# Where the projection matmuls stand in the eight delta rounds of a two-block model

## The chip, the cores and the metric

The kernel runs on one core of one Trainium2 chip. The metric is the device time of one execution in microseconds (us), lower is better. The engines are named as the profile names them: PE (TensorE, with PEld for its weight loads), DVE (VectorE), ACT (ScalarE), POOL (GpSimd) and SP (SyncE, which issues the weight DMAs).

## The reference, cut to what matters

Two transformer-like blocks are applied to 512 positions of width 1024. What the change touches is the gated delta rule in the first block. It runs in two directions over 8 heads, with heads of 128:

```python
lower = where(tri_strict, einsum('cd,sd->cs', k_beta, k) * decay, 0)
sol = triangular_solve(lower, rhs, lower=True, unit_diagonal=True)   # (I + lower)^-1 rhs
v_new = ui - wi @ state
o = qd @ state + qki @ v_new
state = state * exp(gl) + kt.T @ v_new
```

Ahead of it and beside it stand large projections of the same normed input: `proj = h @ w_in` gives the gates, `z`, `q`, `k`, `v` and others, and `y_conv = c @ w_conv_out` follows a depthwise convolution over 31 positions (`depthwise_conv(c, conv_dw_w)`), a layer norm and a silu.

## The kernel before, in words

**Rounds.** The kernel takes 128 positions of 4 heads in both directions at a time: J = 8 problems at once, in 8 rounds R0 to R7 (`delta(R)` on each engine). R0 to R3 are the first four heads, R4 to R7 the last four, and r is the number of the round within its half. In a round PE forms the decay table (L762, pA), the products of k with itself (L767, pB) and of k with q (L773, pA). Then the triangular matrix is inverted by doubling, in 6 levels (`LEVELS`). A level is a product `ub`,`ls` into pC (L746; level 0 uses the identity in `consts`), a copy of it to `yb` by ACT (L1252), then two products, `yb`,`tb` into pC and `tb`,`yb` into pB (L746, in the last level L795), and two subtractions by DVE that renew `ub` (L1723, level 0: L1718, last level: L1726 and L1727 into `en`) and `tb` (L1730). The next level needs the renewed `ub` and a masked matrix `ls` that POOL makes (L2090) between other work of its own. L803 and L810 join the two halves of 64, DVE copies the result (L1747, L1748), and L817, L825 and L827, L835 and L836, and L841 make the new values, the output and the state. DVE adds the output into `oT` (L1757, L1761) and renews the state `st` (L1770).

**Fillers.** A weight unit is a tile of 1024 rows by 128 columns; its product with the 512 positions takes 24 matmuls of 128x512 (L571, into pg), because each fp32 product is made of three fp32r ones (`UNIT` = 24). Four units, 96 matmuls, are handed out over each round: R0 to R3 do the gates, R4 and R5 do `z`, R6 and R7 the convolution's output projection. The table `GAP` says how many of the 96 stand in each of the round's 18 gaps on PE: gap 0 ahead of L773, gap 1 ahead of level 0, gap 2 after level 0, gaps 3 to 12 two to a level (after the first product, and after the other two), gap 13 after L803, gap 14 after L810, gap 15 after L817, gap 16 after the products into pB, gap 17 at the end.

**Taps.** In R0 to R3, called heavy rounds here, DVE also works off the long convolution, tap by tap (L1490, one multiply-add of 128x512). `TAP` gives the number in each gap, 47 a round. They stand in DVE's queue at fixed places: those of gaps 0 and 1 ahead of level 0's `tb` and `ub`, those of gap 17 ahead of the next round's first work (L1693). R4 to R7, the light rounds, have none.

**Weights.** Each unit's weights are split into a rounded part (`w_hi`, ACT, L1020) and a rest (`w_lo`, DVE, L1446), in two slots each. The split for a unit can begin when the unit two before it is finished on PE. DVE does the splits and the evictions at the places that `gap(R, g)` works out from `GAP`: a unit that ends in gap 2 to 16 gets its split at the next odd gap or later, and what ends in gap 15 or 16 is dealt with in gap 17, after the state. In R6 and R7 DVE also evicts the units (`taken`, L1652). pg has two banks, so a unit can begin when the one two before it has been evicted.

Of the kernel before, what the change touches and what calls it, by code (L numbers as in the profile page):

```python
# [34 lines left out]
LEVELS = 6  # L35
# [82 lines left out]
def build(nc, a, out):  # L118

    ctx = ExitStack()  # L120
    with ctx:
# [268 lines left out]
        taps_unit = 8  # L390


        A_, B_ = 4, 4
        GAP = [16, 13, 4] + [A_, B_] * (LEVELS - 1) + [4, 5, 7, 7, 0]
        TAP = [2, 4, 0] + [1, 2] * 2 + [2, 3] * 3 + [0, 4, 5, 6, 5]
        PD = 4
        NORM_AT = 14
        UNIT = 3 * KT
        assert sum(GAP) == 4 * UNIT and taps_unit * (KT - 2) + 3 * HH + 4 * sum(TAP) >= len(TAPS)

# [52 lines left out]
        def parts(R, g):  # L453

            q, end = sum(GAP[:g]), sum(GAP[:g + 1])
            while q < end:
# [984 lines left out]
        def _(dve):  # L1441
# [35 lines left out]
            def taps(count):  # L1477

                for q in range(done_taps[0], min(done_taps[0] + count, len(TAPS))):
                    t, j = TAPS[q]  # L1480
                    src, w = cpad[:, t, j:j + T], vec[:, t, len(VEC) + j:len(VEC) + j + 1]
                    y = csum_in(t)
                    if j == 0:
                        ev_wait(dve, ("gla", t))
                        if 3 <= t < KT - 1:
                            dve.wait_ge(S("tap"), TAPS.index((t - 2, CK - 1)) + 1)
                        ins = dve.tensor_scalar(y, src, w, v("conv_b", t), ALU.mult, ALU.add)
                    else:
                        dve.wait_ge(S("tap"), TAPS.index((t, j - 1)) + 1)
                        ins = dve.scalar_tensor_tensor(y, src, w, y, ALU.mult, ALU.add)  # L1490
                    ins.then_inc(S("tap"), 1)
                done_taps[0] = min(done_taps[0] + count, len(TAPS))
# [164 lines left out]
            def gap(R, g):  # L1657

                n, last = len(GAP), g == len(GAP) - 1
                if g % 2 and g > 1:  # L1660
# [10 lines left out]
                if R < 4:  # L1671
                    taps(TAP[g])

# [571 lines left out]
```

## Time and profile before

| | us |
|---|---|
| median of 3 runs | 2404.41 (2402.77 to 2405.77) |
| the profiled execution | 2404.79 |
| its span | 2402.9 |
| R0 to R3 (248.6 to 530.4) | 66.9, 71.4, 73.7, 69.8 |
| R4 to R7 (641.3 to 881.8) | 56.5, 60.1, 65.1, 58.8 |

A round is counted from the start of L762 to that of the next round's, R3 and R7 to the end of their work on PE. The rounds are 522 us of the span. PE is busy 93% of the span. A matmul's duration in the trace includes its way through the array; what one costs in a row of them is the distance between two starts. A product of fp32 data appears in the trace as two instructions for each one of the program, so that "x32" there is "x16" in the program.

### The profile page before, as it was taken

Reading aid. Unit: us, or ns where it says so; the run is one execution under the profiler, and the core shown is the slowest. Engines: PE = TensorE matmul, PEld = TensorE weight load, DVE = VectorE, ACT = ScalarE, POOL = GpSimd, SP = SyncE. Lnnn points to the kernel's source line nnn. Section 1 sums busy time; section 2 is a strip of 40 time slices with the busy share of each in tenths; the row PEclk is TensorE's granted clock in tenths of the full one; section 3 lists DMA queues with packets and bytes.
Section 4 is the critical chain, followed back from the end, with each engine's and each line's share of the span. In section 5 each row is a group of like instructions: output and inputs, shape, how many; then the busy total and the mean of one; then the engine's idle time right before and its main releaser. Section 6 shows DMA issues by size and latency. Waiting matters only on the chain.

```text
span 2402.9 us, 33875 instructions
## 1 busy us (share of the span) xinstructions
PE 2230.9 (93%) x13850; PEld 1832.4 (76%) x13850; DVE 1304.9 (54%) x1750; ACT 788.9 (33%) x1106; POOL 327.7 (14%) x228
## 2 busy tenths in 40 slices
PE   6999888899899999999999979999988897999996
PEld 4877777778787878888888768888876575888885
DVE  4578798887654446444443354444226835444423
ACT  4345222225433223333322333332223443323221
POOL 0100442130343310100000120000011212000001
PEclk8999899999899999999999979999997986999998
DMA  3232011112111123322232312223221111222321
GB/s 139 82 115 79 28 54 41 45 50 79 36 41 41 54 71 137 122 96 96 96 108 93 105 53 96 96 96 108 96 85 44 36 59 45 97 96 96 111 94 40
DMA packets 54901, 189.68 MB, mean 79 GB/s; under 512 B 6144, under 2 KB 6400, under 8 KB 54784
## 3 DMA queue, kind: packets, MB, share of 16 engines
q1 hardware_dynamic: 51904, 182.75, 22.6%
q10 hardware_dynamic: 2880, 5.24, 0.6%
q8 instruction: 89, 1.46, 0.3%
q14 instruction: 28, 0.23, 0.0%
HBM read 178.53 MB, written 9.44 MB: 78 GB/s over the span
## 4 chain that ended last, share of the span: by engine, by line
PE 77%; DVE 13%; issue 6%; ACT 2%; DMA 1%; SPq 0%; POOL 0%; DVEq 0%; ACTq 0%; POOLq 0%
PE pg L571 65%; PE pC L746 3%; PE pB L602 2%; DVE cpad L1490 2%; DVE w_lo L1446 1%; DVE x L1928 1%; DVE a_lo L1471 1%; PE pB L746 1%; PE pC L609 1%; PE pB L609 1%; DVE oT L1490 1%; DVE sacc L1600 1%; DVE cacc L1490 1%; ACT w_hi L1020 1%; DVE hb L1924 1%
## 5 line engine op out<-in xcount | busy, mean ns | idle before, releaser
L571 PE MATMUL pg<-a_hi,w_hi 128*128 128x512 f32 x1904 | 770.6, 405 | 49.5 <-DVE a_lo L1471 36.2
L571 PE MATMUL pg<-a_hi,w_lo 128*128 128x512 f32 x1904 | 763.8, 401 | 0.0
L571 PE MATMUL pg<-a_lo,w_hi 128*128 128x512 f32 x1904 | 761.9, 400 | 0.0
L1446 DVE TENSOR_TENSOR w_lo<-w_raw,w_hi 128x1024 fp32r<-128x1024 f32 (+3 forms) x299 | 389.1, 1301 | 458.8 <-ACT w_hi L1020 458.7
L1020 ACT ACTIVATE w_hi<-w_raw 128x1024 fp32r<-128x1024 f32 (+3 forms) x299 | 329.6, 1102 | 669.1 <-PE pg L571 648.0
L571 PEld LDWEIGHTS pg<-a_hi,w_hi 128*128 128x128 f32 x1904 | 366.5, 192 | 142.3 <-issue 31.4
L571 PEld LDWEIGHTS pg<-a_hi,w_lo 128*128 128x128 f32 x1904 | 366.6, 193 | 78.4 <-issue 1.3
L571 PEld LDWEIGHTS pg<-a_lo,w_hi 128*128 128x128 f32 x1904 | 367.1, 193 | 74.2 <-issue 0.7
L2073 POOL TENSOR_TENSOR acc<-acc,sq 128x512 f32<-128x512 f32 x64 | 95.1, 1486 | 1368.3 <-ACT sq L1037 1367.4
L571 PE MATMUL pg<-h_hi,w_hi 128*128 128x512 f32 x528 | 208.0, 394 | 0.0
L571 PE MATMUL pg<-h_hi,w_lo 128*128 128x512 f32 x528 | 207.0, 392 | 0.0
L571 PE MATMUL pg<-h_lo,w_hi 128*128 128x512 f32 x528 | 204.9, 388 | 0.0
L1847 DVE TENSOR_TENSOR tmp<-pg,rstd 128x512 f32<-128x512 f32 x66 | 45.7, 692 | 189.3 <-PE pg L571 189.3
L2090 POOL TENSOR_TENSOR ls<-lc,consts 128x512 f32<-128x512 f32 x48 | 74.6, 1561 | 461.5 <-ACT lc L1247 452.9
L571 PEld LDWEIGHTS pg<-h_hi,w_lo 128*128 128x128 f32 x528 | 99.1, 188 | 23.2
L571 PEld LDWEIGHTS pg<-h_lo,w_hi 128*128 128x128 f32 x528 | 99.1, 188 | 22.2
L571 PEld LDWEIGHTS pg<-h_hi,w_hi 128*128 128x128 f32 x528 | 99.3, 188 | 19.7
L1490 DVE SCALAR_TENSOR_TENSOR cpad<-cpad,vec 128x512 f32<-128x512 f32 x120 | 102.0, 911 | 0.2
L1252 ACT ACTIVATE yb<-pC 128x512 f32<-128x512 f32 x40 | 24.0, 599 | 188.1 <-PE pC L746 188.1
L1318 ACT ACTIVATE h_hi<-tmp 128x512 f32 (+1 forms) x66 | 41.7, 632 | 131.7 <-DVE tmp L1851 131.7
L1600 DVE SCALAR_TENSOR_TENSOR sacc<-pad,swt,sacc 128x512 f32<-128x512 f32 x96 | 76.5, 797 | 3.4
L1856 DVE TENSOR_TENSOR h_lo<-tmp,h_hi 128x512 f32 (+1 forms) x66 | 45.7, 692 | 58.3 <-ACT h_hi L1318 58.3
(323 smaller groups left out, 2379.0 us busy)
## 6 DMA issues: line engine op xcount, KB each, us to landing
w_raw<-in_w_gu SPq DMA_DIRECT2D x132, 512.0 KB, 3.3
w_raw<-in_w_in SPq DMA_DIRECT2D x74, 512.0 KB, 3.3
w_raw<-in_w_dn SPq DMA_DIRECT2D x48, 704.0 KB, 4.0
spill_g<-tmp ACTq DMA_DIRECT2D x16, 256.0 KB, 2.0
w_raw<-in_w_co SPq DMA_DIRECT2D x8, 512.0 KB, 3.6
w_raw<-in_w_do SPq DMA_DIRECT2D x8, 512.0 KB, 3.8
w_raw<-in_w_wo SPq DMA_DIRECT2D x8, 512.0 KB, 4.1
w_raw<-in_w_pg SPq DMA_DIRECT2D x8, 512.0 KB, 6.8
```

The lines of the kernel that those rows point to most:

```text
L571: ins = pe.matmul(dst, w_of(w, n % 2, k), b(k), start=first and q == 0, stop=last and q == len(todo) - 1)
L602: ins = pe.matmul(dst[:, c:c + 1], src[:, c * P:(c + 1) * P], ones[:, 0:1], start=q == 0, stop=q == len(srcs) - 1)
L609: ins = pe.matmul(dst[:, c * P:(c + 1) * P], factors[:, c:c + 1].to_broadcast([P, P]), ident, start=True, stop=True)
L746: ins = pe.matmul(dst[s, j, :], lhs[s, j, :], id64[s, :] if rhs is None else rhs[s, j, :], start=True, stop=True)
L1020: act.activation(w_hi[:, n % 2, 0:c], w_raw[:, n % 4, 0:c], ACT.Copy).then_inc(S("w_hi"), 1)
L1446: dve.tensor_tensor(w_lo[:, n % 2, 0:c], w_raw[:, n % 4, 0:c], w_hi[:, n % 2, 0:c].bitcast(F32), ALU.subtract).then_inc(S("w_lo"), 1)
L1490: ins = dve.scalar_tensor_tensor(y, src, w, y, ALU.mult, ALU.add)
L1600: ins = dve.scalar_tensor_tensor(y, src, w, y, ALU.mult, ALU.add)
L1847: dve.tensor_tensor(tmp2[:], bu, rstd[:], ALU.mult).then_inc(S("evD"), 1)
L1856: dve.tensor_tensor(at_m(h_lo), tmp2[:], at_m(h_hi).bitcast(F32), ALU.subtract)\
L2073: pool.tensor_tensor(acc[:], acc[:], sq[:, t % 2, :], ALU.add).then_inc(S("add"), 1)
L2090: pool.tensor_tensor(ls[:, lv % 2].rearrange("p (d h) c -> p d h c", d=2), lc[:].rearrange("p (d h) c -> p d h c", d=2), mask, ALU.mult)\
```

## The change

Two tables of numbers are replaced, and nothing else:

```diff
         taps_unit = 8
 
 
-        A_, B_ = 4, 4
-        GAP = [16, 13, 4] + [A_, B_] * (LEVELS - 1) + [4, 5, 7, 7, 0]
-        TAP = [2, 4, 0] + [1, 2] * 2 + [2, 3] * 3 + [0, 4, 5, 6, 5]
+        GAP = [26, 22, 0] + [0, 0] * (LEVELS - 1) + [10, 10, 14, 14, 0]
+        TAP = [8, 9, 0] + [1, 1] * 5 + [0, 4, 6, 6, 4]
         PD = 4
         NORM_AT = 14
         UNIT = 3 * KT
```

The 96 matmuls of a round now stand as 26 in gap 0, 22 in gap 1, none in gaps 2 to 12, and 10, 10, 14 and 14 in gaps 13 to 16. The 47 taps stand as 8 and 9 in gaps 0 and 1 (2 and 4 before), one in each of gaps 3 to 12 (21 in all before), and 0, 4, 6, 6 and 4 in gaps 13 to 17 (0, 4, 5, 6 and 5 before). All counts and products are the same.

PE in R0, before, one level and the start of the next:

```order
L746 MATMUL pC<-ub,ls 64x64 x16
L571 MATMUL pg<-a_hi,w_lo 128x512
L571 MATMUL pg<-a_hi,w_hi 128x512
L571 MATMUL pg<-a_lo,w_hi 128x512
L571 MATMUL pg<-a_hi,w_lo 128x512
L746 MATMUL pC<-yb,tb 64x64 x16
L746 MATMUL pB<-tb,yb 64x64 x16
L571 MATMUL pg<-a_hi,w_hi 128x512
L571 MATMUL pg<-a_lo,w_hi 128x512
L571 MATMUL pg<-a_hi,w_lo 128x512
L571 MATMUL pg<-a_hi,w_hi 128x512
L746 MATMUL pC<-ub,ls 64x64 x16
```

PE in R0, after, from the end of gap 1 (line numbers are one lower in the changed kernel):

```order
L570 MATMUL pg<-a_hi,w_lo 128x512
L745 MATMUL pC<-consts,ls 64x64 x16
L745 MATMUL pC<-ub,ls 64x64 x16
L745 MATMUL pC<-yb,tb 64x64 x16
L745 MATMUL pB<-tb,yb 64x64 x16
L745 MATMUL pC<-ub,ls 64x64 x16
```

Nothing stands between the products of the levels any more.

DVE in R2, before, from the end of the matrix on (the eight instructions of L1707) to level 1:

```order
L1707 SCALAR_TENSOR_TENSOR en<-pB,gat,en 128x128 x8
L1490 SCALAR_TENSOR_TENSOR cpad<-cpad,vec 128x512 x6
L1716 TENSOR_TENSOR tb<-consts,ls 128x512
L1718 TENSOR_TENSOR ub<-consts,pC 128x512
L1446 TENSOR_TENSOR w_lo<-w_raw,w_hi 128x1024
L1490 SCALAR_TENSOR_TENSOR cpad<-cpad,vec 128x512
L1723 TENSOR_TENSOR ub<-ub,pC 128x512
L1730 TENSOR_TENSOR tb<-tb,pB 128x512
```

and after:

```order
L1706 SCALAR_TENSOR_TENSOR en<-pB,gat,en 128x128 x8
L1489 SCALAR_TENSOR_TENSOR cpad<-cpad,vec 128x512 x17
L1715 TENSOR_TENSOR tb<-consts,ls 128x512
L1717 TENSOR_TENSOR ub<-consts,pC 128x512
L1445 TENSOR_TENSOR w_lo<-w_raw,w_hi 128x1024 x2
L1489 SCALAR_TENSOR_TENSOR cpad<-cpad,vec 128x512
L1722 TENSOR_TENSOR ub<-ub,pC 128x512
L1729 TENSOR_TENSOR tb<-tb,pB 128x512
```

Seventeen taps instead of six now stand ahead of `tb` and `ub`, and both weight splits of the round's first two units stand right behind them.

DVE from the end of R6 to the start of R7, before:

```order
L1761 TENSOR_TENSOR oT<-oT,pA 128x4x128 x2
L1770 SCALAR_TENSOR_TENSOR st<-st,gat,pC 128x128 x8
L1446 TENSOR_TENSOR w_lo<-w_raw,w_hi 128x1024
L1652 TENSOR_TENSOR ya<-pg,tmp_60 128x512
L1693 TENSOR_TENSOR et<-pA,gat 128x512 x2
```

and after:

```order
L1760 TENSOR_TENSOR oT<-oT,pA 128x4x128 x2
L1769 SCALAR_TENSOR_TENSOR st<-st,gat,pC 128x128 x8
L1445 TENSOR_TENSOR w_lo<-w_raw,w_hi 128x1024 x2
L1651 TENSOR_TENSOR ya<-pg,tmp_59 128x512
L1651 TENSOR_TENSOR ya<-pg,tmp_60 128x512
L1692 TENSOR_TENSOR et<-pA,gat 128x512 x2
```

The splits and the evictions (`ya`) of the round's last two units are both at its end now, ahead of the next round's L1692.

## Rows read from the trace of the kernel before

**Rows 1.** The page, part 1: busy time by engine, instructions.
```profile
PE 2230.9 (93%) x13850; PEld 1832.4 (76%) x13850; DVE 1304.9 (54%) x1750; ACT 788.9 (33%) x1106; POOL 327.7 (14%) x228
```

**Rows 2.** By round, R0 to R3, then R5: length, busy PE, PEld, DVE, ACT, POOL, granted clock.
```profile
248.60:315.50 66.90, 59.73 (x737) 50.06 (x737) 59.28 (x80) 20.09 (x27) 24.64 (x16) 0.94 0.12 41
315.50:386.90 71.40, 62.76 (x768) 52.62 (x769) 62.22 (x87) 18.96 (x26) 26.35 (x16) 0.95 0.13 46
386.90:460.60 73.70, 63.43 (x771) 53.18 (x770) 62.95 (x93) 18.96 (x26) 23.58 (x16) 0.93 0.13 44
460.60:530.40 69.80, 59.42 (x755) 49.63 (x753) 63.33 (x94) 17.68 (x25) 20.86 (x14) 0.98 0.14 47
697.80:757.90 60.10, 59.22 (x770) 50.26 (x769) 26.55 (x42) 26.25 (x37) 20.84 (x16) 1.00 0.14 46
```

**Rows 3.** Waits of PE, 641 to 882 us, the light rounds: total, times, longest.
```profile
PE pg L571 <- DVE a_lo L1469: 3.2, 1, 3.2
PE pA L817 <- DVE en L1748: 2.9, 4, 0.7
```

**Rows 4.** Waits of PE, 248 to 531 us, the heavy rounds.
```profile
PE pC L746 <- DVE ub L1723: 10.6, 4, 3.8
PE pC L746 <- DVE ub L1718: 9.7, 3, 4.0
...
PE pA L817 <- DVE en L1748: 4.2, 4, 1.1
```

**Rows 5.** Timeline of PE, one level in R5: start, duration, instruction.
```profile
728.32 1.15 PE L746 MATMUL pC<-ub,ls 64*64 64x64 f32 x32
729.40 0.50 PE L571 MATMUL pg<-a_hi,w_hi 128*128 128x512 f32 x1
...
730.52 1.15 PE L746 MATMUL pC<-yb,tb 64*64 64x64 f32 x32
...
733.68 1.15 PE L746 MATMUL pC<-ub,ls 64*64 64x64 f32 x32
```

**Rows 6.** Timelines of ACT and DVE in the same stretch of R5.
```profile
729.52 0.60 ACT L1252 ACTIVATE yb<-pC 128x512 f32<-128x512 f32 x1 [2.10 <-PE pC L746]
...
731.72 0.69 DVE L1723 TENSOR_TENSOR ub<-ub,pC 128x512 f32<-128x512 f32 x1 [3.13 <-PE pC L746]
...
737.07 0.68 DVE L1726 TENSOR_TENSOR en<-ub,pC 64x512 f32<-64x512 f32 x1 [3.73 <-PE pC L746]
```

**Rows 7.** Timeline of PE in R7: projection matmuls back to back.
```profile
827.06 0.39 PE L571 MATMUL pg<-a_hi,w_lo 128*128 128x512 f32 x1
...
827.97 0.39 PE L571 MATMUL pg<-a_hi,w_hi 128*128 128x512 f32 x1
```

**Rows 8.** Timeline of DVE at the head of R2, then of R1.
```profile
399.12 7.09 DVE L1490 SCALAR_TENSOR_TENSOR cpad<-cpad,vec 128x512 f32<-128x512 f32 x6
...
407.80 0.67 DVE L1718 TENSOR_TENSOR ub<-consts,pC 128x512 f32<-128x512 f32 x1
...
326.36 4.06 DVE L1490 SCALAR_TENSOR_TENSOR cpad<-cpad,vec 128x512 f32<-128x512 f32 x6
```

**Rows 9.** Timeline of POOL at the head of R1.
```profile
327.83 3.71 POOL L2090 TENSOR_TENSOR ls<-lc,consts 128x512 f32<-128x512 f32 x1 [42.48 <-ACT lc L1247]
```

**Rows 10.** Timeline of PE at the head of R2.
```profile
402.36 1.15 PE L746 MATMUL pC<-consts,ls 64*64 64x64 f32 x32 [1.28 <-POOL ls L2090]
...
408.62 1.98 PE L746 MATMUL pC<-ub,ls 64*64 64x64 f32 x32 [3.97 <-DVE ub L1718]
```

**Rows 11.** Timeline of DVE at the start of R2.
```profile
387.13 2.15 DVE L1770 SCALAR_TENSOR_TENSOR st<-st,gat,pC 128x128 f32<-128x128 f32 x8 [0.50 <-PE pC L841]
389.21 1.22 DVE L1446 TENSOR_TENSOR w_lo<-w_raw,w_hi 128x1024 fp32r<-128x1024 f32 x1
```

**Rows 12.** Timeline of PE ahead of R0: the same transposes at either clock.
```profile
232.03 0.60 PE L725 MATMUL pA<-consts,kT 128*128 128x128 f32 x4
...
245.83 1.11 PE L725 MATMUL pA<-consts,kT 128*128 128x128 f32 x4 [0.78 <-DVE kT L1631]
```

## Prediction, made before the changed kernel ran

> **What bounds the kernel now.** I read the page's busy times first: PE is busy 93% of the span [rows 1], so a PE instruction that moves is paid wherever nothing waited before. Then the windows by round: in a light round (R4 to R7) PE is busy for 59.2 of 60.1 us while DVE has only 26.6; in a heavy round (R0 to R3) DVE is busy for 59 to 63 us of 67 to 74 and PE for about as much [rows 2]. So light rounds belong to PE, heavy ones to both. The waits of PE say the same: in the four light rounds it waits 0.7 us ahead of L817 in each, and once for `a_lo` [rows 3]; in the heavy ones it waits for `ub` ahead of level 1 (9.7 us in three rounds), for `ub` inside the inverse (10.6 us in four) and ahead of L817 (4.2 us) [rows 4]. In 522 us of rounds there is little idle time to win, and the question is how much new idle time the bare inverse shows. Last, the timeline of one level gives the prices.
>
> **Prices.** A level lasts 5.36 us, 728.32 to 733.68. A block of four projection matmuls in it takes 1.12 us (729.40 to 730.52) [rows 5]; in a long row a matmul costs 0.91 / 4 = 0.228 us [rows 7], so four are 0.91 and 0.21 us is the price of each switch. PE's own work in a level is 5.36 - 2 x 1.12 = 3.12 us. The bare chain of a level: first product 1.15, ACT starts the copy to `yb` 0.05 after its end and takes 0.60, some 0.12 to PE (an estimate, from the 0.15 between the end of `ub` at 408.47 and PE's start at 408.62 [rows 8, 10]), second product 1.15, DVE starts 0.05 after it, `ub` 0.69, 0.14 to PE: 3.95 us [rows 5, 6]. The product into pB and `tb` fit beside it. So a bare level shows 3.95 - 3.12 = 0.83 us of waiting. The last has two instructions where others have one `ub`: 0.68 more [rows 6].
>
> **Light rounds, each.** Eleven blocks leave the inverse: -11 x 1.12 = -12.3. Their 44 matmuls stand outside: 44 x 0.228 = +10.0; nothing hides 19 of them in gaps 0 and 1, since PE did not wait there. Level 0 to 1 shows 0.05 + 0.69 + 0.15 = 0.9 of waiting, the five levels 5 x 0.83 + 0.68 = 4.8. The 0.7 ahead of L817 is covered by the longer gap 14. Sum +2.7, four times: +10.8 us.
> What the moved splits and evictions add: both `w_lo` of the round's last units are now made in gap 17, a split taking 1.22 [rows 11]. At the head of R6 PE already waits for `a_lo` [rows 3], and DVE comes to it one split later: +1.2. At the head of R7 the first unit needs its bank, which DVE frees in gap 17 behind the state (2.15), two splits (2.4) and in 0.7 of its own (a tap's work) [rows 11], some 5.4 us after the state's product; PE gets there after its 3.5 us of L762 and L767: +2.0. In R4 two splits and the norm's multiplications crowd level 1: +0.8 (0 to 2). Light rounds together +14.8 us. ACT's splits and evictions hide in the time before `yb`, and SP's loads follow units that lie 5.5 us apart as before; I cost both at nothing. If a load were late, a unit would wait, at most the few us that a tile takes to arrive.
>
> **Heavy rounds.** The head is set by DVE: it works off its taps, then `tb`, then `ub` at 407.80, while PE waits 3.97 us [rows 8, 10]. Eleven more taps stand ahead of that. A tap cost 7.09 / 6 = 1.18 in R2, where POOL worked beside it, and 4.06 / 6 = 0.68 in R1 [rows 8]. POOL's first stretch (two `ls`, the masking of `et`) lies beside the first six taps and then waits for `ub`, so I take 0.68 for the added ones: +7.5 (12.9 at 1.18). The second split in gap 17 less one tap there adds 0.5, except in R0. Four heads: 4 x 7.5 + 3 x 0.5 = +31.5. PE's 19 added matmuls, 4.3 us, lie inside the wait, which grows to 9 to 12 us.
> Inverse: five levels from 5.36 to 3.95, plus 0.68: -6.4 each, -25.5. DVE's queue in it: two splits and a tap ahead of level 1's `ub` are 2 x 1.2 + 0.7 = 3.1, beside POOL up to 5.2, against 3.1 of free time; after that three subtractions and two taps are 3.4 to 4.4 a level against 3.95. I take +1.6 a round (0 to 3.8): +6.4. The waits inside, -10.6, go, since the splits that caused them stand elsewhere and four fewer taps stand in each of the later levels' pairs.
> Tail: 25 matmuls x 0.228 = 5.7 each, +22.8; DVE has only one tap more there and now waits for PE. The waits ahead of L817 go, -4.2. After R3 the next stage's first weights are split one split later: +1.2.
> Clock: the lost time is (1 - granted clock) x length, 4.0 + 3.6 + 5.2 + 1.4 = 14.2 us in R0 to R3 [rows 2]. Some 5 us of it follow the waits inside the inverse and go. Behind the longer wait ahead of level 1 PE restarts at 1.2 GHz, where a product takes 1.98 and not 1.15 [rows 10]; a level is then about 2.45 longer (three products). I take one and a half such levels a round, 3.7, against 1.7 now: +8. Net +3.
> Heavy rounds: 31.5 - 25.5 + 6.4 - 10.6 + 22.8 - 4.2 + 1.2 + 3 = +24.6 us.
>
> **Sum.** +14.8 + 24.6 = +39.4 us, on the profiled execution's 2404.8 (span 2402.9 and 1.9 around it; the median is 2404.4): 2444 us.
>
> **A rule of the skill.** In R1 POOL's first `ls` took 3.71 us while DVE's six taps ran at 0.68; in R2 it was the taps that were slow [rows 8, 9]. The Trainium skill (SBUF — State Buffer, Who interferes with whom) says that a DVE instruction with two SBUF inputs contends with a GpSimd instruction that reads SBUF, and that the order of issue decides who is blocked. Both rows fit it, and it speaks against seventeen taps in a row.
>
> **Rivals.**
> *POOL is kept out by the seventeen taps.* Then `ls` for level 0 comes when they end, 11.6 us after the matrix, POOL still has an `ls`, the masking of `et` and the next `ls` ahead of level 2, some 7 us against the 6.5 that PE needs to get there, and sets the later levels too. Up to 1.5 us more a round: 2450. For it: R1's row. Against it: in R2 POOL got in. 18%.
> *The clock stays at 1.2 GHz through the heavy inverses.* Transposes that took 0.60 us took 1.11 after PE had waited, with another wait of 0.78 us in front of them [rows 12]: short waits like those of a bare level did not bring the clock back. All five levels low instead of one and a half: 3.5 x 2.45 x 4 = +34, 2478; if the light inverses fall too, 5 x 2.45 x 4 = 49 on top. Against it: in a low level PE's three products run 5 to 6 us without a wait, and light rounds with waits of 0.7 kept 1.00. 15%, of which 3% for the light ones.
> *Faster.* Taps and POOL no longer collide in the inverse. If heavy rounds belong to DVE alone, with eleven taps each 0.5 us cheaper (5.5 us) and no more idle time on DVE than now, each is 5.4 shorter: -21.6 + 14.8 = -7, 2398. It decides if DVE's idle time (10.8 us in R2 [rows 2]) grows by less than 5.5 - 3.7 = 1.8 us a round. The tail speaks against it: PE gets 5.7 us more there and DVE one tap. 4%.
> *No change*, the two sides cancelling: DVE's idle time would have to grow by just those 1.8 us. 2%.
>
> **How the numbers follow.** 60% for the forecast, 1% for what I don't see. The low end takes DVE's queue at 0 (-6.4), the clock without the added 8, and R4's and R7's terms at half (-2): 2428, and a few us below for the bare chain. The high end takes taps at 1.18 (5.4 x 4 = +22) or the clock rival: 2466 to 2478. Range 2421 to 2480. A measurement of this kernel can tell 0.2%, about 5 us, from no change; the chances are faster 4%, same 2%, slower 94%.
>
> **What would show it.** In the changed kernel's windows light rounds should be 62 to 64 us (R7 about 63.5), heavy ones 70 to 80. The timeline of a light level should read 3.9 to 4.0 us from first product to first product; the waits of PE should name `yb` ahead of L745 with about 0.75 us forty times, and `ub` with 9 to 12 us ahead of level 1 in heavy rounds, and DVE should show 17 taps of about 0.7 there. Wrong would be: heavy heads that do not grow, levels above 5 us in light rounds (the clock), or a POOL that PE waits for at levels 2 to 5.

## The result: 1.6% slower, and the profile after

The changed kernel takes 2441.2 us in the median (2427.2 to 2442.0), the kernel before 2403.6 in the runs beside it: a ratio of 1.0157 (1.0136 to 1.0178). 2444 was forecast, in a range of 2421 to 2480. The profiled execution took 2441.96 us with a span of 2440.1, 37.2 more than before (2402.9).

The page, part 1. PE has the same number of instructions and 12.5 us less busy time in a span that is 37.2 us longer, so what was added is waiting [rows 1]:

```profile
PE 2218.4 (91%) x13850; PEld 1848.1 (76%) x13850; DVE 1304.7 (53%) x1750; ACT 788.3 (32%) x1106; POOL 327.5 (13%) x228
```

The windows by round, R0 to R3 and then R4 to R7 (columns as in [rows 2]):

```profile
250.90:321.50 70.60, 59.69 (x737) 54.01 (x738) 55.81 (x79) 20.07 (x27) 23.85 (x16) 0.87 0.09 31
321.50:399.50 78.00, 61.48 (x770) 55.73 (x769) 62.51 (x87) 18.88 (x26) 23.87 (x16) 0.87 0.13 42
399.50:476.60 77.10, 60.43 (x771) 54.32 (x770) 63.74 (x93) 18.87 (x26) 24.83 (x16) 0.89 0.13 42
476.60:551.70 75.10, 57.73 (x754) 51.53 (x752) 61.66 (x91) 17.59 (x25) 22.39 (x14) 0.91 0.12 43
664.60:725.40 60.80, 53.61 (x736) 47.76 (x737) 30.97 (x46) 19.87 (x27) 22.90 (x16) 1.00 0.06 19
725.40:787.60 62.20, 57.12 (x770) 51.36 (x770) 27.40 (x43) 26.13 (x37) 20.67 (x16) 1.00 0.17 53
787.60:856.10 68.50, 58.97 (x771) 52.31 (x770) 32.35 (x56) 16.73 (x25) 22.07 (x16) 0.98 0.12 39
856.10:919.30 63.20, 55.88 (x754) 49.67 (x752) 27.56 (x48) 14.25 (x20) 18.68 (x14) 1.00 0.18 60
```

R0 to R2 are 3.7, 6.6 and 3.4 us longer than before [rows 2]. R3's window ends with its last work on PE, which in the kernel before came at 529.0, 1.4 ahead of the end of its window in [rows 2] (the 69.8 given for it there hold a wait of 1.4 that belongs to the next stage): 68.4 before, 75.1 now, 6.7 more. The light rounds have 4.3, 2.1, 3.4 and 4.4 us more than the 56.5, 60.1, 65.1 and 58.8 of before.

The waits of PE in the heavy rounds, 250 to 552 us (total, times, longest), against [rows 4]:

```profile
PE pC L745 <- DVE ub L1717: 40.1, 4, 11.7
PE pC L745 <- ACT yb L1251: 13.8, 20, 0.7
PE pC L745 <- DVE ub L1722: 4.5, 7, 1.3
```

And in the light rounds, 664 to 919 us, against [rows 3]:

```profile
PE pC L745 <- ACT yb L1251: 13.7, 20, 0.7
PE pg L570 <- DVE a_lo L1468: 4.5, 2, 4.3
PE pC L745 <- DVE ub L1717: 3.5, 4, 0.9
...
PE pC L745 <- DVE ub L1722: 2.1, 1, 2.1
PE pg L570 <- DVE ya L1651: 1.6, 1, 1.6
```

The wait ahead of level 1 in heavy rounds has gone from 9.7 us in all to 40.1: 5.7 in R0 and 11.1, 11.7 and 11.7 in R1 to R3; `yb`, of which there was no wait in the five levels of R5 before [rows 5], is now waited for in each of the 40 levels, 0.7 us each.

One level on PE in the light round R5 (start, duration, instruction), against [rows 5]. It lasts 755.49 - 751.63 = 3.86 us where it lasted 5.36:

```profile
751.63 1.15 PE L745 MATMUL pC<-ub,ls 64*64 64x64 f32 x32
753.46 1.15 PE L745 MATMUL pC<-yb,tb 64*64 64x64 f32 x32 [0.69 <-ACT yb L1251]
754.45 1.10 PE L745 MATMUL pB<-tb,yb 64*64 64x64 f32 x32
755.49 0.70 PE L745 MATMUL pC<-ub,ls 64*64 64x64 f32 x17
```

DVE and POOL at the head of the heavy round R2, against [rows 8]: seventeen taps in a row, then `tb` and `ub`, with POOL's `ls` beside the first of the taps. They average 15.41 / 17 = 0.91 us.

```profile
412.16 15.41 DVE L1489 SCALAR_TENSOR_TENSOR cpad<-cpad,vec 128x512 f32<-128x512 f32 x17
427.50 0.68 DVE L1715 TENSOR_TENSOR tb<-consts,ls 128x512 f32<-128x512 f32 x1
428.11 0.67 DVE L1717 TENSOR_TENSOR ub<-consts,pC 128x512 f32<-128x512 f32 x1
```

```profile
413.63 3.43 POOL L2089 TENSOR_TENSOR ls<-lc,consts 128x512 f32<-128x512 f32 x2 [46.49 <-ACT lc L1246]
```

PE in R2 from level 1 on. It restarts after 11.67 us at 1.2 GHz (the products take 1.97), and is at 2.4 GHz (1.15) from the second product of level 2, at 437.57, on:

```profile
428.93 1.97 PE L745 MATMUL pC<-ub,ls 64*64 64x64 f32 x32 [11.67 <-DVE ub L1717]
431.58 1.97 PE L745 MATMUL pC<-yb,tb 64*64 64x64 f32 x32 [0.69 <-ACT yb L1251]
...
435.05 1.82 PE L745 MATMUL pC<-ub,ls 64*64 64x64 f32 x32
```

```profile
440.05 1.15 PE L745 MATMUL pC<-ub,ls 64*64 64x64 f32 x32 [0.40 <-DVE ub L1722]
...
444.18 1.15 PE L745 MATMUL pC<-ub,ls 64*64 64x64 f32 x32 [0.21 <-DVE ub L1722]
```

Last, the stretch of R2 from the first product of level 1 to L802 (L803 before), after and then before. It is 8.7 us shorter, at a lower clock:

```profile
428.90:452.80 23.90, 18.87 (x465) 17.70 (x465) 20.77 (x24) 2.99 (x5) 18.06 (x12) 0.84 0.15 47
```

```profile
408.60:441.20 32.60, 30.34 (x505) 24.29 (x505) 26.27 (x33) 4.43 (x7) 16.83 (x12) 0.87 0.13 42
```

### The profile page after: what moved, and what is told of

Its sections match the earlier page's. It is cut to its first block, busy times and chain, and to the rows that moved or that the text cites. A ratio compares the mean times of both kernels' runs of the same rounds, so it can differ in the third digit from the quotient of the medians.

```text
span 2440.1 us, 33875 instructions
## 1 busy us (share of the span) xinstructions
PE 2218.4 (91%) x13850; PEld 1848.1 (76%) x13850; DVE 1304.7 (53%) x1750; ACT 788.3 (32%) x1106; POOL 327.5 (13%) x228
## 3 DMA queue, kind: packets, MB, share of 16 engines
q1 hardware_dynamic: 51904, 182.75, 22.8%
## 4 chain that ended last, share of the span: by engine, by line
PE 80%; DVE 14%; ACT 3%; issue 2%; DMA 1%; SPq 0%; DVEq 0%; ACTq 0%
PE pg L570 66%; PE pC L745 4%; DVE cpad L1489 2%; PE pB L601 2%; PE pB L745 1%; DVE x L1927 1%; DVE w_lo L1445 1%; DVE oT L1489 1%; DVE a_lo L1470 1%; PE pB L608 1%; PE pC L608 1%; ACT yb L1251 1%; DVE sacc L1599 1%; DVE cacc L1489 1%; PE pA L835 1%
## 5 line engine op out<-in xcount | busy, mean ns | idle before, releaser
L570 PEld LDWEIGHTS pg<-a_lo,w_hi 128*128 128x128 f32 x1904 | 365.5, 192 | 73.7 <-issue 0.7
L2089 POOL TENSOR_TENSOR ls<-lc,consts 128x512 f32<-128x512 f32 x48 | 80.4, 1681 | 496.8 <-ACT lc L1246 450.6
L570 PEld LDWEIGHTS pg<-h_hi,w_hi 128*128 128x128 f32 x528 | 99.3, 188 | 19.7
L745 PE MATMUL pC<-ub,ls 64*64 64x64 f32 x1280 | 51.4, 236 | 50.4 <-DVE ub L1717 43.7
L745 PEld LDWEIGHTS pC<-ub,ls 64*64 64x64 f32 x1280 | 47.2, 150 | 53.3 <-issue 52.0
```

Of the source, the lines that this page charges most:

```text
L570: ins = pe.matmul(dst, w_of(w, n % 2, k), b(k), start=first and q == 0, stop=last and q == len(todo) - 1)
L745: ins = pe.matmul(dst[s, j, :], lhs[s, j, :], id64[s, :] if rhs is None else rhs[s, j, :], start=True, stop=True)
L2089: pool.tensor_tensor(ls[:, lv % 2].rearrange("p (d h) c -> p d h c", d=2), lc[:].rearrange("p (d h) c -> p d h c", d=2), mask, ALU.mult)\
```

## The experiments

The theory was the prediction's: the light rounds pay for bare levels, the heavy ones for the seventeen taps ahead of level 1, and both parts add up. The rivals were that only one kind of round pays, that only one of the two tables matters, that POOL kept out by the taps costs extra, and that the clock is the cause. In the experiments the tables may differ by round (`GAPS[R]`). "Old" and "new" are the lists of the diff above; what is not named stays as in the kernel before. Line numbers of their rows are 1 to 10 above those of the kernel before. A round's length is from the start of its first product to that of the next round's; for R3 and R7 it ends with their work on PE. All ratios are against the kernel before, 2400 to 2401.5 us in the median of the runs beside them.

### One half of the rounds at a time

```diff
+        GAPS = [old] * 4 + [new] * 4      # light_only
+        GAPS = [new] * 4 + [old] * 4      # heavy_only, with the new TAP
```

> The new GAP in R4 to R7 alone, the rest as before. Theory (PE owns the light rounds; each shows five waits for yb and pays 44 matmuls outside): +14 us against before, rounds 60.9, 62.2, 68.5 and 63.2 us as in the changed kernel. Rival (the light rounds of the changed kernel were longer because R0 to R3 left ACT, DVE or the loads behind): clearly less than +14, R4 near 57.

Measured: 2418.8 us, 1.0073 (1.0057 to 1.0090), +17.3 us. R5 and R6 are 62.2 and 68.6, as in the changed kernel, and R7 62.5. R4 was 63.4 against 60.8, at a granted clock of 0.95 where the changed kernel had 1.00. The same wait of 2.11 us for `ub` stands in both, ahead of level 3. In the changed kernel the next products still took 1.15; here (line numbers 2 higher) PE came out of it at 1.2 GHz, and the level took 6.1 us instead of 3.9:

```profile
671.36 1.97 PE L747 MATMUL pC<-ub,ls 64*64 64x64 f32 x32 [2.11 <-DVE ub L1724]
```

> The new GAP and TAP in R0 to R3 alone. Theory: the two halves add up, +20 to +23 us against before, with waits for ub ahead of level 1 of about 6, 11, 12 and 12 us. Rival (the halves share a cost, such as the clock or the hand-over between R3 and R4): the two single changes together differ from the +37.5 of the whole by more than 6 us.

Measured: 2423.4 us, 1.0098 (1.0082 to 1.0115), +22 us. The two halves make 17.3 + 22.0 = 39.3 us, where the whole change made 37.6: they add up, and neither kind of round is free. The waits of PE in the heavy rounds of `heavy_only`:

```profile
PE pC L747 <- DVE ub L1719: 29.9, 4, 11.7
...
PE pC L747 <- POOL ls L2091: 8.5, 1, 8.5
```

The 8.5 us are one wait, in R3: there PE did not wait for `ub` behind the taps (only 0.9 us) but for POOL's first `ls`. That is the first rival's mechanism. DVE and POOL in that R3:

```profile
480.26 11.35 DVE L1491 SCALAR_TENSOR_TENSOR oT<-cpad,vec,oT 128x512 f32<-128x512 f32 x17
```

```profile
481.73 12.22 POOL L2091 TENSOR_TENSOR ls<-lc,consts 128x512 f32<-128x512 f32 x2 [43.67 <-ACT lc L1248]
```

In the changed kernel, with the same tables and the same order in R3, POOL's two `ls` took 3.43 and the taps 15.42. From the end of the matrix `en` to the end of `ub` it was 15.1 us with POOL kept out and 16.5 with POOL let in, and the round was 73.9 and not 75.1 us: this mechanism makes the round shorter, not longer. R0 of `heavy_only` was shorter too (67.9 against 70.6), for another reason. POOL was not kept out in it (two `ls` in 2.86, in both kernels), but its first product, L762 of the kernel before, took 2.02 us where it took 3.75 in the changed kernel: PE came into the round at 2.4 GHz and not at 1.2. Its head is 1.7 us shorter, and its levels 0.9.

### One table at a time

```diff
+        GAPS = [new] * 8                  # gap_only, TAP old
+        GAPS = [old] * 8                  # tap_only, TAP new
```

> The new GAP everywhere, TAP as before: six taps ahead of level 0, 21 in the inverse. Theory (heavy rounds: DVE's queue sets whatever stretch its taps stand in): the head's wait for ub shrinks from 12 to about 4 us, but the levels are set by DVE, some 4.5 to 7 us each with 3 to 5 taps in them; both together about as long as in the changed kernel, 2435 to 2447. Rival (only the 17 taps ahead of level 1 make the heavy rounds slow): 25 us less than the changed kernel, about 2415.

Measured: 2448.0 us, 1.0197 (1.0177 to 1.0217), +46.5 us, just above what the theory gave. Its runs lie at 2440 (two, the profiled one among them) and at 2448 to 2449 (three). The rival, that the bare inverse costs little without the seventeen taps, is refuted: the heavy rounds are 72.7, 75.5, 78.5 and 72.9 us, 299.7 in sum against 300.8 in the changed kernel. DVE in its R2, from level 2 on, shows why:

```profile
427.53 0.67 DVE L1724 TENSOR_TENSOR ub<-ub,pC 128x512 f32<-128x512 f32 x1
...
429.91 4.73 DVE L1491 SCALAR_TENSOR_TENSOR cpad<-cpad,vec 128x512 f32<-128x512 f32 x3
434.56 0.68 DVE L1724 TENSOR_TENSOR ub<-ub,pC 128x512 f32<-128x512 f32 x1
...
441.59 0.67 DVE L1724 TENSOR_TENSOR ub<-ub,pC 128x512 f32<-128x512 f32 x1
```

`ub` follows `ub` at 7.0 us (427.53, 434.56, 441.59), because three to four taps stand between, 4.73 / 3 = 1.58 us each in the first level shown. A bare level on PE takes 3.9 to 4.1. With the old taps the bare inverse belongs to DVE: PE waits 16.0 us inside the inverses for `ub`, beside 11.1 ahead of level 1.

> The new TAP, GAP as before. Theory: heads 8 us longer in each of R0 to R3 (32), of which the waits inside the inverse (10.6) and some 5 us of low clock come back: +12 to +18 us against before, about 2418, with a wait for ub ahead of level 1 of about 12 to 15 us in R1 to R3 and none inside. Rival (the moved taps cost nothing, since DVE has the same work): within 5 us of before.

Measured: 2421.2 us, 1.0088 (1.0073 to 1.0103), +19.7 us. The rival (within 5 us of before) is refuted, and the theory's 12 to 18 was somewhat low. Separately the tables cost 46.5 + 19.7 = 66.2, together 37.6: once `GAP` is new, the new `TAP` costs nothing more, since what it adds to the head it takes out of the bare levels and the tail. Over the four heavy rounds, `gap_only` has 86.5 us of heads, 118.5 of levels and 94.7 of tails, the changed kernel 113.0, 97.8 and 90.0. In R2 of `tap_only` (DVE, then POOL):

```profile
412.11 11.34 DVE L1491 SCALAR_TENSOR_TENSOR cpad<-cpad,vec 128x512 f32<-128x512 f32 x17
424.61 1.74 DVE L1717 TENSOR_TENSOR tb<-consts,ls 128x512 f32<-128x512 f32 x1 [1.16 <-POOL ls L2091]
426.65 0.69 DVE L1719 TENSOR_TENSOR ub<-consts,pC 128x512 f32<-128x512 f32 x1 [0.30 <-PE pC L747]
```

```profile
413.58 12.22 POOL L2091 TENSOR_TENSOR ls<-lc,consts 128x512 f32<-128x512 f32 x2 [43.86 <-ACT lc L1248]
```

Here the seventeen taps ran at 11.34 / 17 = 0.67 us each and POOL's two `ls` took 12.22 instead of 3.43. It is the same sequence on DVE up to there as in the changed kernel, where the taps took 15.41. From the end of `en` to the end of `ub` it was 15.15 us here and 16.53 there. A POOL that is kept out thus costs the head 1.4 us less. The prediction had put it at up to 1.5 more a round.

### The taps elsewhere

```diff
+        GAPS = [new] * 8                  # late_taps
-        TAP = [8, 9, 0] + [1, 1] * 5 + [0, 4, 6, 6, 4]
+        TAP = [2, 4, 0] + [1, 1] * 5 + [0, 8, 9, 10, 4]
```

> The changed kernel with TAP's head as before (2 and 4), one tap in each inner gap, and the eleven others in the tail (8, 9, 10 in gaps 14 to 16). Theory (the heavy rounds' loss is the eleven taps ahead of level 1): the wait for ub ahead of level 1 falls from 11.7 to about 4 us in R1 to R3, DVE's tail (31 taps with gap 17, 21 us, beside about 18 us of PE) overruns by some 3 us a round; 12 to 25 us less than the changed kernel, 2416 to 2430. Rival (DVE is full, a tap costs the same wherever it stands): within 5 us of the changed kernel.

Measured: 2416.1 us, 1.0074 (1.0049 to 1.0099), 25 us below the changed kernel and 20 below its second measurement further down (its profiled execution took 2409.2). The heavy rounds of its profile are 274.3 us, 26.5 less than in the changed kernel. The row of R2 in its windows, and PE's wait ahead of level 1 in its heavy rounds:

```profile
384.90:453.60 68.70, 58.95 (x769) 52.93 (x769) 62.41 (x95) 18.87 (x26) 26.30 (x16) 0.98 0.14 47
```

```profile
PE pC L747 <- DVE ub L1719: 7.3, 4, 4.2
```

68.7 us where the changed kernel has 77.1 and the kernel before 73.7. The wait ahead of level 1 falls from 40.1 to 7.3 us. R1 and R2 with a bare inverse are now shorter than before the change. What is left of the loss in the rounds is the light ones (60.9, 62.2, 68.5 for R4 to R6), R0 (68.2 against 66.9) and the hand-over after R3, where PE waits 3.8 us for a split. Of the overrun of 3 us a round that was expected from DVE's full tail one of 4.4 us came, ahead of R1, where PE waits for `oT`; ahead of R2 it is 0.4.

### The clock

This kernel adds work that no result uses: in the wait ahead of level 1 PE multiplies the identity with itself into the bank of pC that is free, 5, 9, 10 and 10 sets of 16 products in R0 to R3.

```diff
+                    if lv == 1 and R < 4:
+                        for _ in range((5, 9, 10, 10)[R]):
+                            warm()        # 16 products id64 x id64 into c1
```

> The changed kernel with extra products of the identity (16 of 64x64, written where the second product of level 1 will overwrite them) put into PE's wait ahead of level 1 in R0 to R3: 5, 9, 10 and 10 such sets, about 1.07 us each. They add nothing to the result. Theory (the wait drops the clock to 1.2 GHz, and level 1 and part of level 2 run at it, some 2.5 to 4 us a round): level 1 at full clock, first products 1.15 instead of 1.97 us, 8 to 14 us less than the changed kernel. Rival (DVE sets the levels at either clock): within 4 us of the changed kernel although the products are short.

Measured: 2432.1 us, 1.0144 (1.0122 to 1.0166). The heavy rounds of its profile are 67.6, 75.7, 75.1 and 73.4 us, 9.0 less than the 300.8 of the changed kernel, and 8.6 of the 9.0 lie in the levels (89.2 against 97.8). PE in R2:

```profile
411.82 6.53 PE L755 MATMUL pC<-consts 64*64 64x64 f32 x218
420.53 1.15 PE L747 MATMUL pC<-ub,ls 64*64 64x64 f32 x32 [2.19 <-DVE ub L1728]
...
425.17 1.15 PE L747 MATMUL pC<-ub,ls 64*64 64x64 f32 x32 [0.71 <-DVE ub L1733]
```

The products of level 1 take 1.15 and not 1.97, and the level 425.17 - 420.53 = 4.64 us and not 6.12. So it is in R0, R2 and R3. In R1 the extra products did not hold the clock: 2.6 us of waiting were left behind them, the first product of level 1 took 1.56 us and the second 1.97. A heavy inverse at full clock takes 21.9 us in these three rounds, against 20.0 for that of R5: what DVE's queue costs it is 1.9 us a round. Against the same 21.9 the inverses of R0 to R3 in the changed kernel are 2.8, 3.8, 1.9 and 1.6 us longer, 10.1 in all. That is what the lower clock costs, where the prediction had 4 x 3.7 = 14.8. By the total time, with the changed kernel at 1.0157 and 1.0139, `warm` can't be told from it, so the 8 to 14 us that the theory expected are seen in the rounds alone.

### Smaller gaps in the light rounds

```diff
+        GAPS = [old] * 4 + [[21, 17, 2] + [2, 2] * 5 + [6, 8, 11, 11, 0]] * 4      # half_light
+        GAPS = [[16, 13, 4] + [8, 0] * 4 + [4, 4] + [4, 5, 7, 7, 0]] * 8           # blocks8
```

> Half the dose, in R4 to R7 alone: two matmuls in each inner gap instead of four or none. Theory (a block of two costs 0.46 + 0.21 us and just covers the 0.7 us wait for yb, so that the exposed wait is a threshold and not in proportion): a level of 4.5 us, rounds within 1 us of before, total within 3 us of before. Rival (in proportion): +7 us.

Measured: 2401.4 us, 1.0015 (1.0002 to 1.0027). R4 and R5 are 56.9 and 60.4 against 56.5 and 60.1. PE in a level of R5:

```profile
726.73 1.15 PE L747 MATMUL pC<-ub,ls 64*64 64x64 f32 x32 [0.60 <-DVE ub L1724]
...
728.57 1.15 PE L747 MATMUL pC<-yb,tb 64*64 64x64 f32 x32
...
731.24 0.97 PE L747 MATMUL pC<-ub,ls 64*64 64x64 f32 x26
```

No wait stands in it (728.57), and it lasts 4.51 us. Two matmuls in each gap cover `yb` everywhere (no wait for it is left in the light rounds) and `ub` in all but one level a round, where 0.6 to 0.9 us are waited for it, 2.5 in all. R6 took 67.5 against 65.1, with `a_lo` and a granted clock of 0.95, which the theory had not foreseen.

> As before, but the eight matmuls of each of levels 1 to 4 stand in one block behind the first product, none between the other two products and the next level. Theory (each switch costs 0.21 us; ub is ready 0.88 us after the second product, and the product into pB takes 0.98, so nothing is exposed): a level of 5.15 instead of 5.36 us in light rounds, 0.8 us a round, 3 us in all, and in heavy rounds more waits for ub since DVE's queue has less slack: -4 to +4 us against before. Rival (a switch is free, 1.12 us was the true price of four matmuls): levels stay at 5.36.

Measured: 2404.9 us, 1.0019 (1.0003 to 1.0034). The levels with one block last 5.15 us instead of 5.35, and the light rounds R4 to R6 are 55.9, 59.4 and 64.3, or 0.6, 0.7 and 0.8 us below those before, as the price of a switch (0.21 a block, four blocks fewer) asks. In the heavy rounds PE waits 16.8 us for `ub` in the second halves of the levels, which have lost their matmuls, against 10.6 [rows 4]. They are 6.9 us longer together (287.3 against 280.4), and the gain of 2.8 in the light rounds is more than used up: +4.8 us in the medians, just above the theory's +4.

### Once more, and what the parts point to

The changed kernel once more:

> The changed kernel once more, beside the two below and the kernel before on one chip. Theory (its time hangs on the granted clock behind the wait ahead of level 1, and is else fixed by the queues): 2437 to 2442 us or 1.014 to 1.017 of before, heads with 17 taps in about 15.4 us. Rival (the first measurement was off by the chip): outside 1.012 to 1.018.

Measured: 2435.8 us, 1.0139 (1.0119 to 1.0158). The rounds R0 to R2 and R4 to R6 are 70.5, 78.0, 77.1 and 60.9, 62.2, 69.6, as in the first profile but for R6, and R2's taps take 15.43. The time is just below what was expected, and well inside what would have put the first one down to the chip.

The three mixes take the new `GAP` in some heavy rounds with late taps, and in the light rounds the eight-blocks of `blocks8`:

```diff
+        t_late = [2, 4, 0] + [1, 1] * 5 + [3, 7, 8, 9, 4]
+        GAPS = [g_old, g_new, g_new, g_old] + [g_light] * 4    # mix_middle, TAP by round alike
+        GAPS = [g_new, g_new, g_new, g_new] + [g_light] * 4    # mix_all
+        GAPS = [g_new, g_new, g_new, g_old] + [g_light] * 4    # mix_first3
```

> R1 and R2 with the new GAP, six taps ahead of level 0, one in each inner gap, 3, 7, 8, 9 and 4 in gaps 13 to 17; R0 and R3 as before; R4 to R7 with the eight inner matmuls of levels 1 to 4 in one block. Theory: DVE owns the heavy rounds, and in late_taps R1 and R2 took 68.9 and 68.6 us against 71.4 and 73.7 before; three taps into the wait of 2.0 us ahead of L1747 take up to 2 us more off each, and the light rounds keep the 0.6 to 0.8 us of blocks8: -8 to -13 us against before, 2389 to 2394. Rival (PE owns the heavy rounds too, and the gain in late_taps was the clock's luck): within 4 us of before.

Measured: 2388.4 us, 0.9946 (0.9925 to 0.9968), faster than both kernels. R1 is 66.8 and R2 69.7, against 71.4 and 73.7 before.

> The same with R0 and R3 too in the new form. Theory: R0 has no wait that the new form removes (68.2 against 66.9 in late_taps) and R3's end waits some 3.8 us for a split behind DVE's taps: +1 and +3 us against mix_middle, 2393 to 2398. Rival (the form is better everywhere where taps stand): faster than mix_middle.

Measured: 2391.8 us, 0.9963 (0.9948 to 0.9979), not faster than `mix_middle` and below what was expected. R0, of which nothing was expected, went to 63.9 from 66.9. R3 took 70.5 with the wait of the next stage for a split, and gained nothing.

> R0 to R2 in the form of mix_all, R3 as before, light rounds as in both. In the profiles R0 took 63.9 us in mix_all and 66.9 in mix_middle, R3 70.5 against 69.8. Theory (the gains of the rounds are separate and add up): 3 to 4 us less than mix_middle, 0.991 to 0.994 of before, with R0 64, R1 and R2 67 to 70, R3 70. Rival (R0's 63.9 came with the granted clock of that one execution or is given back in R1): as mix_middle, 0.994 to 0.996.

Measured: 2386.2 us, 0.9944 (0.9922 to 0.9966). R0 to R2 of `mix_first3`:

```profile
245.90:309.90 64.00, 54.00 (x737) 47.90 (x737) 57.72 (x80) 20.04 (x27) 24.60 (x16) 1.00 0.10 34
309.90:377.20 67.30, 58.65 (x768) 52.71 (x769) 63.29 (x87) 18.87 (x26) 25.14 (x16) 0.97 0.15 48
377.20:446.90 69.70, 60.49 (x771) 54.35 (x770) 64.47 (x93) 18.87 (x26) 24.67 (x16) 0.93 0.14 47
```

R0 takes 64.0 us at a granted clock of 1.00, where it was 66.9 at 0.94 before. In total time this kernel can't be told from `mix_middle`, and most of the gain in R0 is not the tables' doing. The first product of R0 in `mix_first3` and in `late_taps`, which has the same head:

```profile
245.91 2.02 PE L767 MATMUL pA<-consts,gat 128*128 128x128 f32 x16 [0.83 <-ACT vtok L1196]
```

```profile
247.76 3.75 PE L763 MATMUL pA<-consts,gat 128*128 128x128 f32 x16 [0.78 <-ACT vtok L1192]
```

In `mix_first3`, `mix_all` and `heavy_only` PE comes into R0 at 2.4 GHz, in the other eleven profiles, those of the kernel before and of the changed one among them, at 1.2. All that stands ahead is the same in all of them. The head of R0 is 18.5 us in the one case and 20.8 in the other (`late_taps`), so 2.3 of the 3.0 us are the clock that the round started with: the rival about the clock was not ruled out. The gains of R1 and R2 have no such difference behind them: both start at 2.4 GHz in the kernel before and in the mixes, and R2's 4.0 us in `mix_first3` come at the same granted clock, 0.93.

## Why the prediction was right, step by step

**Sum.** +39.4 us were forecast and +37.6 measured in the medians (+37.2 in the spans). The size of each step could be checked in the profile. The rounds and the hand-over make 14.2 + 20.4 + 1.3 = 35.9 us of the spans' 37.2. R0 also began 2.4 us later, in a stretch where both kernels are the same, and the rest of the span gave 1.1 back; that part is chance.

**A bare level.** 3.95 us were worked out for it from rows of the kernel before; it lasts 3.86 in R5. The wait for `yb` is 0.69 where about 0.75 was said.

**Light rounds,** +14.8 forecast, +14.2 measured:

| | forecast | measured |
|---|---|---|
| R4 | 2.7 + 0.8 | 4.3 |
| R5 | 2.7 | 2.1 |
| R6 | 2.7 + 1.2 | 3.4 |
| R7 | 2.7 + 2.0 | 4.4 |

The reasons of the terms show in the waits: R4's is the one wait of 2.1 for `ub` (L1722), R6's is that for `a_lo`, which went from 3.2 to 4.3, R7's is `ya` with 1.6, beside 0.7 in level 4 for which the trace names no releaser. The common part was 2.1 and not 2.7, which makes 2.4 us less over the four rounds. R4's term was 2.2 and not 0.8, R6's 1.3 and not 1.2, R7's 2.3 and not 2.0, which makes 1.8 more. That the sum comes within 0.6 us is in part luck.

**Heavy rounds,** +24.6 forecast, +21.7 measured (with the hand-over). From the starts of PE's instructions each round splits into a head (to the first product of level 1), the levels (to L803, now L802) and the tail, the four rounds together:

| | before | after | measured | forecast |
|---|---|---|---|---|
| heads | 81.5 | 112.9 | +31.4 | +31.5 |
| levels | 125.4 | 97.8 | -27.6 | -25.5 + 6.4 - 10.6 + 3 = -26.7 |
| tails | 73.5 | 90.1 | +16.6 | 22.8 - 4.2 = +18.6 |
| wait after R3 | 1.4 | 2.7 | +1.3 | +1.2 |

The heads came out right for a reason that was only half right. The eleven added taps were taken at 0.68 each beside a POOL that has stopped. In fact POOL and DVE shared some 6.8 us at the head in R2 (3.43 of `ls`, then 3.38 of masking), the taps took 15.41 instead of the 7.09 + 7.5 = 14.6 of the sum, and `tb`, which had taken 1.75 us beside POOL, took 0.68. The one makes up for the other. What was not seen is that moving `tb` behind the end of POOL's work makes it 1 us cheaper. (The 12.9 for the same taps at 1.18 should be 13.0.)

The levels came out right by two errors that cancel. Before, the four heavy inverses were 19.1 us longer than four like R5's, and the prediction took 10.6 + 5 + 4 x 1.7 = 22.4 out for that. It put back 4 x 3.7 for the low clock and 6.4 for DVE's queue, 21.2 us, and measured are 10.1 and 4 x 1.9 = 7.7, 17.8 in all (from `warm`). In the later levels three taps fewer stand, not four.

**The clock** was forecast in a net of +3 with about one and a half levels a round at 1.2 GHz. R2 shows level 1 with 6.12 us (435.05 - 428.93) and level 2 with 440.05 - 435.05 = 5.00, which `warm` has as 4.64 and 4.58 at 2.4 GHz: 1.9 us in R2 and 2.5 a round over the four, where 3.7 were said. The slow levels overlap with what DVE's queue would have cost anyway. The lost time (1 - granted clock) x length rose from 14.2 to 9.2 + 10.1 + 8.5 + 6.8 = 34.6 us. Some 15 us of it lie inside the waits ahead of level 1 and cost nothing there, which is why that number must not be read as a price.

**The rivals.** *POOL kept out* did not happen in the changed kernel. It happened in R2 of `tap_only` and in R3 of `heavy_only`, and it was cheaper there: the taps then run at 0.67. The mechanism exists, its price had the wrong sign. On the rule cited from the Trainium skill (SBUF — State Buffer, Who interferes with whom), that the order of issue decides who is blocked: with the same tables and the same order, and with POOL's `ls` starting 1.39 us behind the end of `en` each time, POOL's pair took 3.43 us in R3 of the changed kernel and 12.22 in R3 of `heavy_only`. Both outcomes exist, and neither the program's order nor that distance tells which. *The clock at 1.2 GHz through the inverses* did not come: the first product of level 3 is at 1.15 again in all four rounds. It did fall a second time in two of them, for about one level: in level 3 of R0 behind waits of 0.95 and 0.69 us (the products into pB take 1.92) and in level 4 of R1 behind 1.26 and 0.69, but not in level 3 of R3 behind 1.29. So the rival's point, that short waits in the inverse can bring the clock down, has something in it. *Faster*: the condition was that heavy rounds belong to DVE alone and its idle time does not grow. DVE's idle time in R2 went from 73.70 - 62.95 = 10.8 to 77.10 - 63.74 = 13.4 us, 2.6 more where 1.8 was the limit, and DVE's busy time did not fall by the 5.5 either (63.0 and 63.7). Still, this rival held a truth that the prediction gave no weight: with the taps in the tail, where PE has 25 matmuls more, R1 and R2 do become shorter than before (66.8 and 69.7). The prediction looked at the tail as pure loss (+5.7 a round, "DVE has only one tap more there and now waits for PE"), and that idle DVE time is what `late_taps` and the mixes use.

**What stays open.** Which of the two, POOL or DVE, is blocked in a given round could not be told from the program, and no run settles it. Nor is it shown why the same wait is followed by 1.2 GHz in one kernel and by 2.4 in another. The total times of one kernel scatter by up to 18 us (2392.2 to 2409.8 for `blocks8`; the profiled execution of `mix_first3` was its fastest), while the rounds of the two profiles of the changed kernel agree to 0.1 us but for R6. Much of the scatter lies outside the rounds. R0 starts at 245.9 to 251.6 us in the fourteen profiles, and from R7's last work on PE to the end they have 1513.5 to 1521.6 us, both in stretches where the programs are the same. In the last one the granted clock goes along with it: 0.949 or 0.950 in the three profiles that take 1520.8 to 1521.6, 0.954 or 0.955 in the four that take 1513.5 to 1515.4. What makes it differ is open.

## What to carry to other kernels

Filler work between the steps of a dependent chain costs only its switches (0.21 us a block here) and covers the chain's latency. Taking it out is free only as far as that latency is below what the fillers took: two matmuls of 0.23 us in each gap were nearly enough here, with none a level showed 3.86 - 3.12 = 0.7 us of waiting. When fillers of one engine move, ask first what the other engine's fillers now do to the chain: the new `GAP` lost in every heavy round with the old taps and with the new ones, and gained 4.0 to 4.6 us in R1 and in R2 once the taps stood where PE had become long (`mix_middle`). Put the work of each engine where the other one is long, and not ahead of the step that the other one waits for.

## What was not expected of the hardware

- The same seventeen multiply-adds on DVE took 15.42 us beside a POOL that got its turn (two `ls` in 3.43) and 11.35 beside one that did not (two `ls` in 12.22), in R3 of two kernels with the same instructions in that round. The head was 1.4 us shorter in the second case.
- `tb`, one multiply or subtraction of 128x512 on DVE, took 0.68 us with POOL idle and 1.74 with POOL at work; `ub`, which reads one operand from PSUM, took 0.67 with POOL idle and 0.69 with POOL at work (R2 of `tap_only`).
- A wait of 0.7 us in every level of 3.9, with single ones of 0.9, 1.6 and 2.1, left the granted clock at 1.00 in R4, R5 and R7 of the changed kernel. The same wait of 2.11 us in R4 of `light_only` was followed by products of 1.97 us. After a wait of 11.67 us PE's products took 1.97 us in level 1 and 1.82 at the start of level 2, with waits of 0.7 between them, and then 1.15 again.
